# The second layer's output projection cut in eight weight units, the DeltaNet half of it placed inside the GLA norm chain

## The chip, the core and the metric

The kernel runs as one program on one core of a Trainium2 chip. The metric is the device time of one execution in us. The engines are PE (TensorE, matrix multiplication), DVE (VectorE), ACT (ScalarE), POOL (GpSimd) and SP (SyncE, which here only issues DMAs). Each runs its own instruction list in order and waits on semaphores for the others.

## The reference, cut to what matters

A decoder trunk of two layers runs once on 272 prompt tokens (16 meta tokens and 256) and on 8 sample groups of 4 tokens; the kernel puts them side by side as T = 304 columns. Layer 0 mixes with retention and mLSTM and has a gated feed-forward block. Layer 1 mixes with gated DeltaNet (heads "c") and GLA (heads "d"), projects both through one matrix `w_out1`, and ends with a mixture of experts, top 2 of 8:

```python
def _mixer_odd(x, state, segments, p):
    proj = x @ p['w_in1']
    qkv_c, z_c, b_c, a_c, q_d, k_d, v_d, r_d, lr_d = _split(proj, SPLITS1)
    ...
    o_c, s_gdn = _run_segments(_gdn_step, s_gdn, (qc, kc, vc, beta, g), segments)
    y_c = _merge(_head_norm(o_c, p['gdn_norm_g'], rms=True)) * jax.nn.silu(z_c.astype(f32))
    ...
    o_d, s_gla = _run_segments(_gla_step, s_gla, (qd, kd, vd, _heads(log_alpha, HD)), segments)
    y_d = _merge(_head_norm(o_d, p['gla_norm_g'])) * jax.nn.silu(r_d.astype(f32))
    y = jnp.concatenate([y_c, y_d], -1).astype(x.dtype) @ p['w_out1']

    # in _trunk, layer 1:
    x = _layer_norm(ALPHA * x + h, p['ln1_mix_g'], p['ln1_mix_b'])
    f = _moe(x, p['moe_w_router'], p['moe_b_router'], p['moe_w_gate'], p['moe_w_up'], p['moe_w_down'])
```

The final states of DeltaNet and GLA are outputs too, for the prompt and for every sample group.

## The kernel before

Activations are held as feature rows by token columns: 8 blocks of 128 features, 304 columns. Large products are done in a split form: ACT copies an operand to a "hi" part in a reduced type, DVE subtracts it from the raw one to give a "lo" part, and PE adds three matmuls (hi·hi, lo·hi, hi·lo; L612 to L614 in the helper `mm3`). So every weight tile passes SP (DMA), ACT (hi), DVE (lo) and PE in that order. The whole order of the program is written out by hand, engine by engine; nothing schedules it. Semaphores carry short names: `g_` is DeltaNet, `l_` GLA, `b_` the second output projection, `n1m_` the layer norm after it, `u_` a weight unit of the experts.

Layer 1 goes through these places. In the input projection PE takes 28 weight units of 24 matmuls (loop `unit1`), with the steps of DeltaNet's triangular solve between them. Then DeltaNet's outputs are formed (`g_o`) and evicted; `norm("g_", ...)` on DVE and ACT makes its 4 rows of `mix`, while PE makes four products for the new states, and DVE's `state_update` (one TENSOR_TENSOR L2025 and two L2027) adds each to the state. GLA follows: transposes of values (`l_vt`, copied to `vtl`) and keys (`l_kt`, to `ktl`), scores (`l_qk`), masked by DVE to `attl`, chunk products (L1163, L1166), from which DVE makes the running sums `sc` (L2481, L2483, signal `l_sc`), and four outputs (L1177 to L1182). They are evicted, and the GLA norm chain begins: head means on PE (L715), centring on DVE, squares on ACT, head variances on PE (L722), logarithm and exponential on ACT, gain on DVE, split to hi and lo. Between these PE does the four GLA state products (L1193), and DVE adds them (`l_update`, L2491 and L2493).

Only then comes the output projection: `w_out1` in two groups of 2 MB in `wring`, split into four `w_parts` of 2048 words each, 192 matmuls for 8 feature blocks with all 8 blocks of `mix` as input. `residual1` adds the old x (L2157), the layer norm sums on PE (L731), subtracts the mean (L2164), squares on ACT (L1470), sums again (L739), and the router starts (L1209). ACT copies the first two units, `for n in range(2): unit_hi(n)` (L1656), ahead of `layer_norm("n1m_", False)`.

The experts' weights are loaded by SP in units of 1.4 MB into five buffers. The first needs all earlier stores out of the way:

```python
            sp.wait_ge(*at("l_out", 1))
            sp.wait_ge(*at("st_all", 16 * 18))
```

The last of these 18 stores is that of the GLA states, which POOL issues (L1823) after `l_stu` 4, DVE's fourth `l_update`.

## Time and profile before

| what | value |
|---|---|
| time of the runs | 1535.31 us median of 3 (1535.15 to 1537.86) |
| profiled execution, its own time | 1540.06 us |
| its span in the trace | 1538.2 us |
| PE busy | 1418.4 us (92%) |
| DVE, ACT, POOL busy | 977.4, 744.9, 240.2 us |
| granted PE clock, mean | 0.924 of full speed |

A busy share is an average over stages with different limits; what a change in one stage is worth is read from the waits in that stage. "[1.67 <-ACT zT L1630]" at the end of a timeline row says that the engine was idle 1.67 us before it, and what it waited for. A PEclk of 1.00 is 2.4 GHz, 0.50 is 1.2 GHz.

### The profile page before, as it was taken

The numbers are of one execution on the slowest core, as the hardware profiler recorded it, in microseconds if no ns is written. First come the engines' busy times: TensorE is split into PE (matmuls) and PEld (weight loads), VectorE is DVE, ScalarE is ACT, GpSimd is POOL, SyncE is SP. The second block draws the span as 40 slices with busy tenths as digits, with TensorE's granted clock in tenths as the row PEclk, the third lists the DMA queues.
The fourth block names the chain that finished last, engine by engine and source line by source line (L and its number), as shares of the span: only waits on it lengthen the run. The fifth ranks groups of instructions, "written<-read, shape, count | busy, mean of one in ns | idle before, by whom it ended". The sixth has DMA issues, their size and how long they took to land.

```text
span 1538.2 us, 18458 instructions
## 1 busy us (share of the span) xinstructions
PE 1418.4 (92%) x7933; PEld 1237.4 (80%) x7933; DVE 977.4 (64%) x939; ACT 744.9 (48%) x622; POOL 240.2 (16%) x166
## 2 busy tenths in 40 slices
PE   7999999799999889998898766999999999999994
PEld 6898886799999678997686655887888888888882
DVE  4434465554553658743526556687988888788886
ACT  4434322432332566312303335566777778677771
POOL 0210302000000000001212040000000103356452
PEclk9999987899999989997657868999999999999998
DMA  7422624645424122202223437898999995400003
GB/s 256 144 95 83 231 96 140 201 129 177 147 83 144 46 83 83 87 29 56 68 76 103 176 133 282 309 382 334 377 396 377 387 375 213 160 28 14 15 14 98
DMA packets 80890, 254.81 MB, mean 166 GB/s; under 512 B 11568, under 2 KB 47700, under 8 KB 68008
## 3 DMA queue, kind: packets, MB, share of 16 engines
q1 hardware_dynamic: 66008, 224.53, 40.1%
q0 software_dynamic: 14800, 29.10, 6.2%
q8 instruction: 63, 1.03, 0.3%
q14 instruction: 19, 0.16, 0.0%
HBM read 306.09 MB, written 16.70 MB: 210 GB/s over the span
## 4 chain that ended last, share of the span: by engine, by line
PE 80%; DVE 7%; ACT 5%; DMA 5%; issue 2%; POOL 0%; POOLq 0%; SPq 0%; DVEq 0%; ACTq 0%
PE PS L612 11%; PE PS L614 10%; PE PS L613 10%; PE PS L1271 7%; PE PS L1273 7%; PE PS L1276 7%; DMA u_raw<-in_w_moe 4%; PE PS L592 3%; PE PS L1294 3%; PE PS L1295 3%; PE PS L1298 3%; PE PS L1008 2%; ACT u_hi L1656 1%; PE PS L677 1%; PE PS L1182 1%
## 5 line engine op out<-in xcount | busy, mean ns | idle before, releaser
L2508 DVE TENSOR_TENSOR u_lo<-u_raw,u_hi 128x2816 fp32r<-128x2816 f32 x144 | 441.9, 3089 | 110.1 <-ACT u_hi L1656 109.7
L1656 ACT ACTIVATE u_hi<-u_raw 128x2816 fp32r<-128x2816 f32 x144 | 367.7, 2561 | 183.4 <-DMA u_raw<-in_w_moe 114.4
L612 PE MATMUL PS<-x_in_hi,p_hi 128*128 128x304 f32 x480 | 158.1, 329 | 10.6 <-DVE x_in_lo L1898 10.5
L613 PE MATMUL PS<-x_in_lo,p_hi 128*128 128x304 f32 x480 | 148.1, 309 | 0.0
L614 PE MATMUL PS<-x_in_hi,p_lo 128*128 128x304 f32 x480 | 148.1, 309 | 0.0
L1271 PE MATMUL PS<-u_hi,xg_hi 128*128 128x512 f32 x576 | 142.6, 380 | 5.5 <-DVE xg_lo L2587 3.1
L1273 PE MATMUL PS<-u_hi,xg_lo 128*128 128x512 f32 x576 | 141.6, 378 | 0.0
L1276 PE MATMUL PS<-u_lo,xg_hi 128*128 128x512 f32 x576 | 140.2, 375 | 0.0
L612 PE MATMUL PS<-x_out_hi,w_parts 128*128 128x304 f32 x416 | 128.2, 308 | 9.4 <-DVE x_out_lo L1898 9.4
L614 PE MATMUL PS<-x_out_hi,w_parts 128*128 128x304 f32 x416 | 127.2, 306 | 0.0
L613 PE MATMUL PS<-x_out_lo,w_parts 128*128 128x304 f32 x416 | 126.7, 305 | 0.0
L1271 PEld LDWEIGHTS PS<-u_hi,xg_hi 128*128 128x128 f32 x576 | 103.4, 191 | 28.1 <-DVE xg_lo L2587 3.9
L1844 POOL DMA_INDIRECT u_raw<-in_w_moe,wpick x48 | 108.8, 2267 | 105.9 <-PE PS L1276 75.1
L1913 DVE TENSOR_TENSOR p_lo<-p_raw,p_hi 128x1024 fp32r<-128x1024 f32 x40 | 50.1, 1257 | 113.4 <-ACT p_hi L1358 113.4
L1273 PEld LDWEIGHTS PS<-u_hi,xg_lo 128*128 128x128 f32 x576 | 102.5, 190 | 21.6
L1276 PEld LDWEIGHTS PS<-u_lo,xg_hi 128*128 128x128 f32 x576 | 101.6, 188 | 21.1
L1294 PE MATMUL PS<-u_hi,ht_hi 128*128 128x512 f32 (+1 forms) x288 | 107.9, 378 | 1.2 <-issue 1.2
L612 PEld LDWEIGHTS PS<-x_in_hi,p_hi 128*128 128x128 f32 x480 | 94.1, 196 | 17.8 <-DVE x_in_lo L1898 10.5
L1295 PE MATMUL PS<-u_hi,ht_lo 128*128 128x512 f32 (+1 forms) x288 | 106.7, 374 | 0.0
L613 PEld LDWEIGHTS PS<-x_in_lo,p_hi 128*128 128x128 f32 x480 | 94.3, 196 | 0.4
L614 PEld LDWEIGHTS PS<-x_in_hi,p_lo 128*128 128x128 f32 x480 | 93.7, 195 | 0.0
L612 PEld LDWEIGHTS PS<-x_out_hi,w_parts 128*128 128x128 f32 x416 | 79.8, 192 | 11.5 <-issue 8.8
(545 smaller groups left out, 2501.6 us busy)
## 6 DMA issues: line engine op xcount, KB each, us to landing
u_raw<-in_w_moe SPq DMA_DIRECT2D x96, 1408.0 KB, 8.5
p_raw<-in_w_first SPq DMA_DIRECT2D x40, 512.0 KB, 3.5
p_raw<-in_w_second SPq DMA_DIRECT2D x28, 512.0 KB, 3.5
dring<-in_ffn_w_down SPq DMA_DIRECT2D x8, 1408.0 KB, 6.8
wring<-in_ffn_w_gate SPq DMA_DIRECT2D x9, 1024.0 KB, 5.6
wring<-in_ffn_w_up SPq DMA_DIRECT2D x9, 1024.0 KB, 8.1
wring<-in_w_out SPq DMA_DIRECT2D x2, 2048.0 KB, 7.7
o_rows<-zT POOLq DMA_DIRECT2D x6, 512.0 KB, 5.7
```

The costliest lines, as they stand in the source:

```text
L612: mm(out, w[0], x[0], start=start, stop=False)
L613: mm(out, w[0], x[1], start=False, stop=False)
L614: return mm(out, w[1], x[0], start=False, stop=stop)
L1271: mm(PSf[:, a:a + w], x_hi, w_hi[:, a:a + w], start=k == 0, stop=False)
L1273: mm(PSf[:, a:a + w], x_lo, w_hi[:, a:a + w], start=False, stop=False)
L1276: last = mm(PSf[:, a:a + w], x_hi, w_lo[:, a:a + w], start=False, stop=k == GUK - 1)
L1294: mm(o, h[0][:, j, :], w_hi[:, a:a + w], start=j == 0, stop=False)
L1295: mm(o, h[1][:, j, :], w_hi[:, a:a + w], start=False, stop=False)
L1656: A(uhi[n % HIS][:], uraw[n % RAW][:], COPY).then_inc(s("u_hi"), 1)
L1844: pool.indirect_dma_start(uraw[n % RAW][:], None, w_rows, bass.IndirectOffsetOnAxis(ap=wpick[:, o, u:u + 1], axis=0), bounds_check=NE * UP ...
L1913: TT(plo[n % PRAW][:], praw[n % PRAW][:], phi[n % PHI][:].bitcast(F32), SUB).then_inc(s("a_lo"), 1)
L2508: TT(ulo[n % RAW][:], uraw[n % RAW][:], uhi[n % HIS][:].bitcast(F32), SUB).then_inc(s("u_lo"), 1)
```

## The change

The second projection now goes in 8 units of 24 matmuls. The first four (n = 0 to 3) take blocks 0 to 3 of `mix` (DeltaNet), are placed by `first_half` between the PE steps of the GLA norm chain, and are added to x by DVE at once (`partial1`). The last four take blocks 4 to 7 (GLA) and stand where the projection stood. The units have their own raw buffers `oraw` (four in `arena`, four in `wring`), which is why GLA's `ktl`, `vtl` and `attl` leave `arena`. The 12 value transposes and their copies move from the DeltaNet states into the input projection (n = 25, 26). The key transposes and scores use other PSUM banks, and stand among the DeltaNet state products. DVE's wait for the store of the DeltaNet prompt state (`st_gp`) moves from the GLA masks to the residual. The four GLA outputs now wait for both halves of the running sums.

```diff
+        orw_at = [a_at + 1024 * r for r in range(4)] + [wring_at + 4096 + 1024 * r for r in range(4)]
+        ohi_at = [st_at + 6144, st_at + 7168, a_at + 4096]
+        oraw = [nc.alloc_sbuf_tensor_at(f"o_raw{n}", [128, KT, 128], F32, offset=SBUF0 + 4 * at_) for n, at_ in enumerate(orw_at)]
+        olo = [split(f"o_lo{n}", at_, [128, KT, 128]) for n, at_ in enumerate(orw_at)]
+        ohi = [split(f"o_hi{n}", at_, [128, KT, 128]) for n, at_ in enumerate(ohi_at)]
...
-        ktl = carve(arena, 6080, 768, 3, 256)
-        vtl = carve(arena, 6848, 1536, 3, 512)
-        attl = carve(arena, 8384, HT, 4, T)
+        ktl = carve(wring, 1216, 768, 3, 256)
+        vtl = carve(cst, N1 + 7, 1536, 3, 512)
+        attl = carve(wring, 1984, HT, 4, T)
...
-        GPAIRS = [(4, 7), (5, 7), (0, 1), (2, 3)]
+        GPAIRS = [(4, 7), (4, 7), (0, 1), (2, 3)]
...
-        LCHUNK = [(1, 2, 3), (4, 5, 6)]
-        LPAIRS = [(4, 5), (6, 7), (0, 1), (2, 3)]
-        LNB = {"n0m_": 2, "n0f_": 0, "n1m_": 4}
+        LCHUNK = [(2, 3, 4), (5, 0, 1)]
+        LQK = [5, 4, 0, 1]
+        OUTB = [6, 7, 0, 1, 2, 3, 4, 5]
+        LPAIRS = [(4, 5), (0, 1), (2, 3), (4, 5)]
+        LNB = {"n0m_": 2, "n0f_": 0, "n1m_": 6}
...
+            def out1(n):
+
+                if n % NHALF == 0:
+                    sp.wait_ge(*at(("g_o", "l_qk")[n // NHALF], 4))
+                if n >= NHALF:
+                    sp.wait_ge(*at("b_hi", n - NHALF + 1))
+                sp.dma_start(oraw[n][:], I["w_second"][NU1 + n]).then_inc(s(f"b_ld{n % NHALF}"), 16)
...
             for n in range(RAW):
-                if n == RAW - 1:
-                    sp.wait_ge(*at("b_lo", 4))
+                if n < NHALF:
+                    sp.wait_ge(*at("b_hi", NHALF + n + 1))
                 unit_load(n)
...
+            def out1(n, bank, free, between=None):
+
+                w, x = (ohi[n % 3], olo[n]), xsplit["out"]
+                pe.wait_ge(*at("b_lo", n + 1))
+                for j in range(2):
+                    d = 2 * (n % NHALF) + j
+                    pe.wait_ge(*free(d))
+                    for k in range(4):
+                        kx = k + (4 if n >= NHALF else 0)
+                        last = mm3(PS[:, bank(d), 0:T], [w[0][:, 4 * j + k, :], w[1][:, 4 * j + k, :]], [x[0][:, kx, :], x[1][:, kx, :]], k == 0, k == 3)
...
+                    last.then_inc(s("b_pe"), 1)
...
+                if n == 25:
+                    pe.wait_ge(*at("g_tok_d", 6))
+                    pe.wait_ge(*q_evicted(23))
+                    for i in range(2):
+                        tokens(4 + i, i, 20).then_inc(s("l_vt"), 1)
+                if n == 26:
+                    pe.wait_ge(*at("l_tok", 1))
+                    tokens(4, 2, 20).then_inc(s("l_vt"), 1)
             pe.wait_ge(*at("q_ev", len(REST)))
             pe.wait_ge(*at("sv_ev", len(ORDER)))
-            pe.wait_ge(*at("g_tok_d", 6))
+            pe.wait_ge(*at("l_tok", 3))
...
-            pe.wait_ge(*at("g_stu", 2))
-            for i, b in enumerate((4, 5, 7)):
-                tokens(b, i, 20).then_inc(s("l_vt"), 1)
-            pe.wait_ge(*at("g_stu", 4))
-            pe.wait_ge(*at("l_tok", 1))
-            pe.wait_ge(*at("l_dqk", 1))
-            for i, (a, n) in enumerate(TILES):
-                for p in range(2):
-                    last = tr(PS[0:n, 3 + i // 2, 256 * (i % 2) + 128 * p:256 * (i % 2) + 128 * p + 128], k2[:, p, a:a + n], 128)
-            last.then_inc(s("l_kt"), 1)
-            pe.wait_ge(*at("l_tok", 6))
...
+            def first_half(n):
+                out1(n, lambda d: 6 + d % 2, lambda d: at("b_ev", d - 1) if d >= 2 else at(*(("g_pst", 1), ("g_stu", 2))[d]))
+
            g_state(0)
+            head_vars("g_")
+            pe.wait_ge(*at("g_stu", 1))
+            g_state(1)
+            pe.wait_ge(*at("l_dqk", 1))
+            pe.wait_ge(*at("g_rstd", 1))
+            g_state(2)
+            for i, (a, n) in enumerate(TILES):
+                if i == 2:
+                    pe.wait_ge(*at("g_stu", 2))
+                for p in range(2):
+                    last = tr(PS[0:n, 5 - i // 2, 256 * (i % 2) + 128 * p:256 * (i % 2) + 128 * p + 128], k2[:, p, a:a + n], 128)
+            last.then_inc(s("l_kt"), 1)
+            g_state(3)
+            pe.wait_ge(*at("l_tok", 6))
+            l_scores(0)
+            l_scores(1)
+            pe.wait_ge(*at("g_stu", 3))
+            l_scores(2)
+            l_scores(3)
+            pe.wait_ge(*at("l_vb0", 1))
+            pe.wait_ge(*at("g_stu", 4))
+            pe.wait_ge(*at("l_att", 2))
+            l_chunks(0)
+            pe.wait_ge(*at("l_att", 4))
+            l_chunks(1)
+            pe.wait_ge(*at("ld_stG", 32))
+            pe.wait_ge(*at("l_sc", 2))
+            for h in range(H):
+                l_out(h)
+            head_means("l_")
+            pe.wait_ge(*at("xlo", 9))
+            first_half(0)
+            head_vars("l_")
+            first_half(1)
+            l_state(0)
+            first_half(2)
+            pe.wait_ge(*at("l_rstd", 1))
+            l_state(1)
+            first_half(3)
+            l_state(2)
+            pe.wait_ge(*at("l_stu", 1))
+            l_state(3)
+
+            OUTF = [at("b_ev", 7), at("b_ev", 8)] + [at("l_stu", 2)] * 2 + [at("l_stu", 3)] * 2 + [at("l_stu", 4)] * 2
             pe.wait_ge(*at("xlo", 10))
-            group(0, xsplit["out"], lambda t: [at("l_stu", 2)])
-            group(1, xsplit["out"], lambda t: [at("l_stu", 4)], between=mean_between("n1m_", 4 * GEND))
-            ln_sum("n1m_", [6, 7], "b_ev", 4 * GEND)
+            for n in range(NHALF, 2 * NHALF):
+                out1(n, lambda d: OUTB[d], lambda d: OUTF[d])
+                if n == 7:
+                    ln_sum("n1m_", range(4), "b_ev", 16)
+            ln_sum("n1m_", range(4, KT), "b_ev", 16)
...
+            def out1_hi(n):
+
+                act.wait_ge(*at(f"b_ld{n % NHALF}", 16 * (n // NHALF + 1)))
+                if n == 2:
+                    act.wait_ge(*at("g_state_pe", 4))
+                if n >= 3:
+                    act.wait_ge(*at("b_pe", 2 * (n - 2)))
+                A(ohi[n % 3][:], oraw[n][:], COPY).then_inc(s("b_hi"), 1)
...
+            def value_tokens(i):
+                n = TILES[i][1]
+                act.wait_ge(*at("l_vt", i + 1))
+                A(vtl[0:n, i, :], PS[0:n, 4 + i % 2, :], COPY).then_inc(s("l_tok"), 1)
...
+                if n == 26:
+                    act.wait_ge(*at("st_conv", 16))
+                    value_tokens(0)
+                    value_tokens(1)
+            value_tokens(2)
...
+            out1_hi(0)
...
-            for i, (a, n) in enumerate(TILES):
-                act.wait_ge(*at("l_vt", i + 1))
-                A(vtl[0:n, i, :], PS[0:n, (4, 5, 7)[i], :], COPY).then_inc(s("l_tok"), 1)
             act.wait_ge(*at("l_kt", 1))
             for i in range(3):
                 n = TILES[i][1]
-                A(ktl[0:n, i, :], PS[0:n, 3 + i // 2, 256 * (i % 2):256 * (i % 2) + 256], COPY).then_inc(s("l_tok"), 1)
+                A(ktl[0:n, i, :], PS[0:n, 5 - i // 2, 256 * (i % 2):256 * (i % 2) + 256], COPY).then_inc(s("l_tok"), 1)
+            out1_hi(1)
             x_hi("out", 0, mix, at("g_out", 1))
+            out1_hi(2)
             for h in range(H):
                 act.wait_ge(*at("l_o", h + 1))
                 A(zT[:, h, :], PS[:, h, 0:T], COPY).then_inc(s("l_oev"), 1)
-            norm("l_", lambda: proj_hi(0))
+            norm("l_", lambda: out1_hi(3))
+            out1_hi(4)
             x_hi("out", 1, mix, at("l_out", 1))
-            act.wait_ge(*at("l_state_pe", 4))
-            proj_hi(1)
-            proj_hi(2)
-            proj_hi(3)
+            for n in range(5, 2 * NHALF):
+                out1_hi(n)
...
+            def out1_lo(n):
+
+                dve.wait_ge(*at("b_hi", n + 1))
+                TT(olo[n][:], oraw[n][:], ohi[n % 3][:].bitcast(F32), SUB).then_inc(s("b_lo"), 1)
+
+            def partial1(d):
+                dve.wait_ge(*at("b_pe", d + 1))
+                STT(xT[:, d, :], xT[:, d, :], ALPHA, PS[:, 6 + d % 2, 0:T], MUL, ADD).then_inc(s("b_ev"), 1)
...
-                for u in range(4):
-                    if u < 2:
-                        proj_lo(2 + u)
-                    for k in (2 * u, 2 * u + 1):
-                        g = k // 4
-                        dve.wait_ge(*at("b_pe", 4 * g + k % 4 + 1))
-                        STT(zT[:, k, :], xT[:, k, :], ALPHA, PS[:, 4 * ((g + 1) % 2) + k % 4, 0:T], MUL, ADD).then_inc(s("b_ev"), 1)
+                for d in range(KT):
+                    dve.wait_ge(*at("b_pe", 9 + d))
+                    TT(zT[:, d, :], xT[:, d, :], PS[:, OUTB[d], 0:T], ADD).then_inc(s("b_ev"), 1)
...
-            norm("g_", 0, 12, "gdn", rms=True, prepare=lambda: g_update(0))
-            for h in range(1, H):
-                g_update(h)
+            norm("g_", 0, 12, "gdn", rms=True, prepare=lambda: (g_update(0), out1_lo(0)))
+            g_update(1)
+            x_lo("out", 0, mix, 9)
+            out1_lo(1)
+            g_update(2)
+            g_update(3)
...
-                if h == 0:
-                    dve.wait_ge(*at("st_gp", 16))
...
+            for h in range(H):
+                l_att(h)
+            out1_lo(2)
+            l_chunks(0)
+            l_chunks(1)
...
-            x_lo("out", 0, mix, 9)
-            norm("l_", 4, 24, "gla", prepare=lambda: (l_update(0), proj_lo(0)))
+            def before_rstd():
+                partial1(0)
+                partial1(1)
+                out1_lo(3)
+                partial1(2)
+                partial1(3)
+
+            norm("l_", 4, 24, "gla", prepare=before_rstd)
+            l_update(0)
+            x_lo("out", 1, mix, 10)
+            partial1(4)
+            partial1(5)
+            out1_lo(4)
             l_update(1)
-            x_lo("out", 1, mix, 10)
+            partial1(6)
+            partial1(7)
+            out1_lo(5)
             l_update(2)
             l_update(3)
-            proj_lo(1)
+            out1_lo(6)
+            out1_lo(7)
+            dve.wait_ge(*at("st_gp", 16))
```

On DVE, at the DeltaNet states: before, the second to fourth state update (L2025, L2027) stand one behind the other, and the prompt state (L2462) follows; the masks come after it. `stA` is the DeltaNet state, `vb`, `stu` and the like in brackets are the semaphores waited for.

```order
L2025 TENSOR_TENSOR stA<-stA,arena 128x8x128 [waits state_pe]
L2027 TENSOR_TENSOR stA<-stA,PS 128x4x128 [waits dve_chain]
L2027 TENSOR_TENSOR stA<-stA,PS 128x4x128
L2025 TENSOR_TENSOR stA<-stA,arena 128x8x128 [waits state_pe]
L2027 TENSOR_TENSOR stA<-stA,PS 128x4x128 [waits dve_chain]
L2027 TENSOR_TENSOR stA<-stA,PS 128x4x128
L2025 TENSOR_TENSOR stA<-stA,arena 128x8x128 [waits state_pe]
L2027 TENSOR_TENSOR stA<-stA,PS 128x4x128 [waits dve_chain]
L2027 TENSOR_TENSOR stA<-stA,PS 128x4x128
L2462 SCALAR_TENSOR_TENSOR arena<-arena,PS 128x128 x4
```

Now the split of `mix` (L1938) and of a weight unit of the projection (L1943) stand between the second update and the third:

```order
L2069 TENSOR_TENSOR stA<-stA,arena 128x8x128 [waits state_pe]
L2071 TENSOR_TENSOR stA<-stA,PS 128x4x128 [waits dve_chain]
L2071 TENSOR_TENSOR stA<-stA,PS 128x4x128
L1938 TENSOR_TENSOR x_out_lo<-mix,x_out_hi 128x1216 [waits xhi]
L1943 TENSOR_TENSOR o_lo_94<-o_raw_86,o_hi_102 128x1024 [waits hi]
L2069 TENSOR_TENSOR stA<-stA,arena 128x8x128 [waits state_pe]
L2071 TENSOR_TENSOR stA<-stA,PS 128x4x128 [waits dve_chain]
L2071 TENSOR_TENSOR stA<-stA,PS 128x4x128
L2069 TENSOR_TENSOR stA<-stA,arena 128x8x128 [waits state_pe]
L2071 TENSOR_TENSOR stA<-stA,PS 128x4x128 [waits dve_chain]
L2071 TENSOR_TENSOR stA<-stA,PS 128x4x128
L2505 SCALAR_TENSOR_TENSOR arena<-arena,PS 128x128 x4
```

The third and fourth update, the prompt state and the masks moved behind L1938, which waits for ACT (`xhi`).

On PE, in the same place: before, the last two DeltaNet state products (L1130, L1132) are followed by value transposes (`cc,proj`) and key transposes (`cc,wring`).

```order
L1130 MATMUL PS<-dring,arena 128x128 [waits vb,rstd]
L1132 MATMUL PS<-dring,arena 128x512 x2
L1130 MATMUL PS<-dring,arena 128x128 [waits vb]
L1132 MATMUL PS<-dring,arena 128x512 x2
L592 MATMUL PS<-cc,proj 128x128 [waits stu]
L592 MATMUL PS<-cc,proj 128x128 x7
L592 MATMUL PS<-cc,proj 48x128 x4
L592 MATMUL PS<-cc,wring 128x128 [waits l_dqk,tok_act,stu]
L592 MATMUL PS<-cc,wring 128x128 x3
L592 MATMUL PS<-cc,wring 48x128 x2
L1153 MATMUL PS<-wring 128x128 [waits tok_act]
```

Now the key transposes stand ahead of the fourth state product, and the last two wait for a state update (`stu`):

```order
L1132 MATMUL PS<-dring,arena 128x128 [waits vb,rstd,l_dqk]
L1134 MATMUL PS<-dring,arena 128x512 x2
L594 MATMUL PS<-cc,wring 128x128 x4
L594 MATMUL PS<-cc,wring 48x128 [waits stu]
L594 MATMUL PS<-cc,wring 48x128
L1132 MATMUL PS<-dring,arena 128x128 [waits vb]
L1134 MATMUL PS<-dring,arena 128x512 x2
L1141 MATMUL PS<-wring 128x128 [waits tok_act]
```

So ACT's key copies, which stand ahead of `xhi` on ACT, wait for the second state update.

On ACT, from the GLA norm to the layer norm: before, one copy of `mix` (L1343), three weight parts (L1351) and two expert units (`u_hi`, L1656) stand ahead of the layer norm's squares (L1470).

```order
L1456 ACTIVATE zT<-zT 128x1216 [waits act_chain]
L1343 ACTIVATE x_out_hi<-mix 128x1216 [waits out]
L1351 ACTIVATE w_parts<-wring 128x2048 [waits ring0,state_pe]
L1351 ACTIVATE w_parts<-wring 128x2048 [waits proj_pe,ring1] x2
L1656 ACTIVATE u_hi_98<-u_raw_88 128x2816 [waits fill0,proj_pe]
L1656 ACTIVATE u_hi_99<-u_raw_89 128x2816 [waits fill1]
L1470 ACTIVATE mix<-zT 128x608 [waits normcent] x4
```

Now it is five weight units (`o_hi`, L1382) and the same two expert units, ahead of the squares (L1501):

```order
L1487 ACTIVATE zT<-zT 128x1216 [waits act_chain]
L1382 ACTIVATE o_hi_102<-o_raw_89 128x1024 [waits proj_pe,fill0]
L1373 ACTIVATE x_out_hi<-mix 128x1216 [waits out]
L1382 ACTIVATE o_hi_103<-o_raw_90 128x1024 [waits proj_pe,fill1]
L1382 ACTIVATE o_hi_101<-o_raw_91 128x1024 [waits proj_pe,fill2]
L1382 ACTIVATE o_hi_102<-o_raw_92 128x1024 [waits proj_pe,fill3]
L1696 ACTIVATE u_hi_117<-u_raw_107 128x2816 [waits fill0,proj_pe]
L1696 ACTIVATE u_hi_118<-u_raw_108 128x2816 [waits fill1]
L1501 ACTIVATE mix<-zT 128x608 [waits normcent] x4
```

The two expert units still stand directly ahead of the squares; the copies before them became shorter and more.

## Rows read from the trace of the kernel before

**Rows 1.** Windows of all engines: stretch, length, busy (count) each, PEclk, DMA share, GB/s.
```profile
660.00:692.00 32.00, 31.61 (x253) 31.19 (x251) 13.55 (x19) 5.31 (x9) 0.09 (x1) 1.00 0.05 17
782.00:808.00 26.00, 25.84 (x119) 25.50 (x119) 4.78 (x11) 1.27 (x3) 0.00 (x0) 0.51 0.02 7
833.60:860.40 26.80, 26.80 (x187) 26.27 (x187) 11.01 (x12) 3.83 (x2) 3.66 (x5) 1.00 0.84 295
876.00:892.00 16.00, 16.00 (x84) 15.40 (x84) 6.71 (x28) 3.49 (x6) 0.00 (x0) 0.51 0.12 48
```

**Rows 2.** Timeline of PE, input projection: start us, us, engine, line, operation, tiles, [idle before].
```profile
649.60 1.31 PE L592 MATMUL PS<-cc,mix 128*128 128x128 f32 x12
...
692.12 1.28 PE L1079 MATMUL PS<-proj,arena 16*128 16x304 f32 x4 [0.51 <-ACT proj L1604]
```

**Rows 3.** Timeline of ACT, copies at the DeltaNet states.
```profile
765.63 0.59 ACT L1635 ACTIVATE arena<-PS 48x512 f32<-48x512 f32 x1 [0.24 <-PE PS L592]
768.60 0.91 ACT L1639 ACTIVATE arena<-PS 128x256 f32<-128x256 f32 x3 [2.38 <-PE PS L592]
769.41 1.21 ACT L1343 ACTIVATE x_out_hi<-mix 128x1216 fp32r<-128x1216 f32 x1
```

**Rows 4.** Timeline of DVE, from the second DeltaNet state update to the running sums.
```profile
761.44 1.28 DVE L2027 TENSOR_TENSOR stA<-stA,PS 128x512 f32<-128x512 f32 x2
...
767.55 1.11 DVE L2462 SCALAR_TENSOR_TENSOR arena<-arena,PS 128x128 f32<-128x128 f32 x4
773.24 0.42 DVE L2471 TENSOR_TENSOR arena<-PS,cst 128x256 f32<-128x256 f32 x1 [4.58 <-DMA out_prompt_gdn<-arena]
...
778.39 0.59 DVE L2481 COPY dring<-PS 64x128 f32<-64x128 f32 x2 [2.32 <-PE PS L1166]
...
785.81 1.43 DVE L1898 TENSOR_TENSOR x_out_lo<-mix,x_out_hi 128x1216 fp32r<-128x1216 f32 x1
```

**Rows 5.** Timeline of POOL, behind the DeltaNet prompt state.
```profile
769.96 1.05 POOL L1810 TENSOR_TENSOR dring<-arena,cst 48x512 f32<-48x512 f32 x1
```

**Rows 6.** Timeline of PE, from the GLA chunks to the head variances.
```profile
775.43 2.08 PE L1163 MATMUL PS<-arena 64*128 64x256 f32 x8
...
782.16 1.54 PE L1177 MATMUL PS<-arena 48*128 48x48 f32 x6 [2.06 <-DVEq L2485]
...
808.43 4.40 PE L715 MATMUL PS<-zT,cc 128*128 128x304 f32 x8
...
815.59 2.31 PE L722 MATMUL PS<-zT,cc 128*128 128x304 f32 x8 [0.63 <-ACT zT L1452]
817.83 1.98 PE L1193 MATMUL PS<-dring,arena 48*128 48x512 f32 x4
```

**Rows 7.** Timeline of DVE, the GLA gain, state updates three and four.
```profile
823.85 1.87 DVE L2014 SCALAR_TENSOR_TENSOR mix<-zT,vec,proj 128x304 f32<-128x304 f32 x4
...
829.68 1.21 DVE L2491 TENSOR_TENSOR stB<-stB,proj 64x1024 f32<-64x1024 f32 x1
...
833.49 1.30 DVE L2493 TENSOR_TENSOR stB<-stB,PS 64x512 f32<-64x512 f32 x2
```

**Rows 8.** SP's issue of the second expert unit.
```profile
843.63 0.81 SPq L568 DMA_DIRECT2D u_raw<-in_w_moe  x1
```

**Rows 9.** DMA issues by line at 843.6: queue, count, KB, median us to landing.
```profile
u_raw<-in_w_moe SPq DMA_DIRECT2D x1, 1408.0 KB, 9.3
```

**Rows 10.** Timeline of ACT, expert units behind the projection.
```profile
860.61 4.99 ACT L1656 ACTIVATE u_hi<-u_raw 128x2816 fp32r<-128x2816 f32 x2 [13.42 <-PE PS L614]
```

**Rows 11.** Timeline of PE, layer norm to the router.
```profile
860.41 2.21 PE L731 MATMUL PS<-zT,cc 128*128 128x304 f32 x8
866.25 4.36 PE L739 MATMUL PS<-mix,cc 128*128 128x304 f32 x16 [3.63 <-ACT mix L1470]
875.97 6.10 PE L1209 MATMUL PS<-proj,xT 128*128 128x8 f32 x32 [5.35 <-DVE xT L2176]
```

**Rows 12.** The page's DMA issues: tiles, queue, count, KB each, median us to landing.
```profile
p_raw<-in_w_second SPq DMA_DIRECT2D x28, 512.0 KB, 3.5
```

More of the change, by code:

```diff
@@ L556, in _ @@
                 unit1(n)
-            for g in range(GEND):
-                group(g)
+            for n in range(2 * NHALF):
+                out1(n)
             def unit_load(n):
@@ L667, in out_unit @@
                     last.then_inc(s("a_pe"), 1)
+                    if between is not None:
+                        between(4 * j + 3)
+            def out1(n, bank, free, between=None):
[7 more added lines that the diff above has]
+                        last = mm3(PS[:, bank(d), 0:T], [w[0][:, 4 * j + k, :], w[1][:, 4 * j + k, :]], [x[0][:, kx, :], x[1][:, kx, :]], k == 0, k == 3)
+                        if between is not None and k < 3:
+                            between(4 * j + k)
+                    last.then_inc(s("b_pe"), 1)
                     if between is not None:
```

93 lines of the change are left out of this document (22 added, 71 removed).

## The prediction

> **What bounds the kernel now.** I read the profile page first, then the chain that ended last, windows, and the timelines of each engine. All rows are from one execution of 1540.06 us; the runs have their median at 1535.31 us, 4.75 us less. Sums below are differences in that execution and are carried to the median unchanged.
>
> Up to 692 us PE is the bound of the input projection: 31.61 of 32 us busy at full clock [rows 1]. Anything put on PE there is paid in full, and its end hands over to ACT and back with 0.51 us idle [rows 2]. Then the chain goes through small steps in which PE, ACT and DVE wait for one another [rows 3 to 6]: the end of the DeltaNet states on DVE, a DMA wait of 4.58 us before the GLA masks, chunk products, running sums, and at 782.16 the four GLA outputs. These take until 808.43, 26.3 us on PE alone, at a clock of 0.51 [rows 1, 6]. From 808.43 the GLA norm chain alternates between engines, the states are updated [rows 7], and the projection keeps PE busy until 860.4 [rows 1]. Beside it SP loads the first expert units, the second at 843.63, landed after 9.3 us [rows 8, 9]; ACT copies two of them when the projection ends [rows 10], then squares for the layer norm, and PE sums [rows 11]. What comes later moves with that point.
>
> I follow one mark: the start of the layer norm's second sums on PE, 866.25 (L739). Write H for the start of the head means (L715): now 808.43, so the mark is at H + 57.8.
>
> **The change part by part.**
>
> *Transposes sooner.* 12 value transposes go into the input projection. 12 of the same form took 1.31 us there [rows 2]. ACT's copy of the third value tile, 0.59 us [rows 3], now stands between the last eviction and PE's L1079, which waits for it. Cost 1.9 us. Their old place was a gap of PE before the state updates ended, so taking them out of it gives nothing by itself.
>
> *DVE among the DeltaNet states.* The second update ends at 761.44 + 1.28 = 762.7 [rows 4]. Now PE waits for it with the last two key transposes (0.3 us, between 0.11 each at full clock [rows 2] and double), ACT copies the keys (0.91), one weight unit (1.0, from 1.21 us for 1216 columns to 1024) and `mix` (1.21) [rows 3], with handovers at 0.1: DVE is idle for 3.7 us. It then splits `mix` (1.43 us [rows 4]) and a unit (1.2, by 1024/1216). Together 6.3 us before the third update, which followed at once before. The prompt state ended at 767.55 + 1.11 = 768.66 and ends at 775.0.
>
> *Masks, chunks, sums.* The masks no longer wait for the DMA, 4.58 us [rows 4]; what is late next is POOL's value block, behind the issue of the prompt state's store. It ended at 769.96 + 1.05 = 771.0 [rows 5], 2.35 after the prompt state: now 777.35. DVE's masks and one unit (four pairs from 775.0 at about 0.5 each, and 1.2) end at 778.2, beside that. From the chunk products' start at 775.43 [rows 6] to the sums at 778.39 [rows 4] took 2.96 us: now 780.3. The outputs started after the first half of the sums; now they wait for both, which take until the 785.81 row [rows 4], 7.4 us: now 787.7 instead of 782.16 [rows 6], 5.5 late. With the 1.9 above, the outputs and H are 7.4 us late. The outputs themselves are unchanged.
>
> *Projection inside the norm chain.* A unit of 24 matmuls costs 3.3 us: 26.80 us held 187 instructions, 8 of them sums that took about 2.2 us (rows 11 show such a group), leaving 24.6 us for 179 [rows 1, 11]. Head means are 4.4, head variances 2.25, a GLA state product 2.0 [rows 6]. On PE: 4.4 + 3.3 + 2.25 + 3.3 + 2.0 + 3.3 + 2.0 = H + 20.6. The fourth unit then waits for DVE's `partial1`(4). The variances start at H + 7.7, and the gain's end came 10.1 after their start, 823.85 + 1.87 - 815.59 [rows 6, 7]: H + 17.8. Behind it DVE has a state update (1.21 + 1.30 = 2.5 [rows 7]), the split of `mix` (1.43) and the partial sum (0.5): H + 22.2. PE: that unit 3.3, two state products 4.0, H + 29.5, then four units, the last matmul at H + 42.7. Now it is at 860.4 = H + 52.0. Eight sums come after it, twice 2.21 [rows 11]: the mean is there at H + 47.1.
>
> *What decides: the fourth GLA update.* From H + 22.2 DVE does another partial sum, a unit, an update, two partial sums, a unit, then updates three and four: 0.5 + 1.2 + 2.5 + 1.0 + 1.2 + 5.0 = H + 33.6. Before, it ended at 833.49 + 1.30 = 834.8 = H + 26.4 [rows 7]. Behind it are queued POOL's store of the GLA states, SP's wait for all stores, and the expert loads. The second unit landed at 843.63 + 9.3 = 852.9, 18.1 after the update [rows 8, 9]; now H + 51.7. ACT copies it, half of 4.99 [rows 10], until H + 54.2; the squares stand behind that. Before, the copies ended at 865.6 = H + 57.2, and PE followed 0.65 later [rows 10, 11]. So the mark comes 3.0 earlier after H, not the 9 that the projection frees. Net 7.4 - 3.0 = 4.4 us later.
>
> *The clock at the mark.* PE is then idle from H + 47.1 to H + 54.8, 7.7 us; now it is 3.63 us, and the 16 sums ran at full clock in 4.36 [rows 11]. After an idle time of 5.35 the next stretch ran at 0.51 [rows 1, 11]. By the first row the sums cost nothing more; all at half clock they would cost 4.4 more, since 8 took 4.40 at the head means [rows 6]. I take 2.2: the first 8 at half clock, the rest full, as the head means and what followed them did. The Trainium skill ("TensorE: Matmul & The Clock Gate", section "What's actually happening") says that the default state is throttled and that activity releases the throttle. By that rule the sums start at half clock; the row of 5.35 agrees, the row of 3.63 does not show it.
>
> Edits at nothing: the four early weight loads (the same form lands after 3.5 us [rows 12]; as late as 9.3, as an expert unit [rows 9], they would delay DeltaNet's norm by up to 5.8; nothing else is queued there, and before 745 nothing waits for them, so no gain: I take 0); DVE's `st_gp` wait at the residual (the store is long done); banks and places in memory. The copies of units five to eight lie beside PE's units.
>
> Sum: 1.9 + 5.5 - 3.0 + 2.2 = +6.6 us: 1546.7 in the profiled execution, 1541.9 by the median.
>
> **The rivals.**
>
> 1. *Expert units are not in the way* (not slower). If the second unit lands 11.8 us after the fourth update instead of 18.1, the squares follow the mean at once: 47.1 + 0.7 for the subtraction + 0.7 for a square = H + 48.5 instead of 57.8. Then 7.4 - 9.3 = -1.9, 1533.4 us. For it speaks that the DMA queues are nearly idle in that stretch; against it that the store, its wait and the 9.3 us are all measured. It decides below a landing of about 14 us.
> 2. *The GLA outputs run at full clock* (faster): half of 26.3 us, 13.1, would go: 1528.8. Dense matmuls come before and after; but the outputs followed dense work before as well and stayed at 0.51 [rows 1].
> 3. *No loss of clock* at the mark: +4.4, 1539.7.
> 4. *More at half clock*: the first unit behind the head means (3.3 more) and all 16 sums (2.2 more): +12.1, 1547.4.
> 5. *The half is not hidden*: PE does not fit it between the chain's steps, since the chain waits for PE more than PE for it. That is in my sum for H + 22.2; if DVE were never late there, updates would end 1.6 sooner, 1540.3.
>
> **How the numbers follow.** Forecast with its own spread (rival 5 within it) 0.47; rival 3 0.18; rival 4 0.12; rival 1 0.16; rival 2 0.07. Below 0.2%, 3.1 us, a measurement of this kernel can't be told from no change. Slower by more: the forecast, rival 4 and most of rival 3, 0.75. Faster by more: rival 2 and a part of rival 1, 0.11. Within: 0.14. The range 1533.0 to 1546.5 takes in rival 1 and most of rival 4; the slower cases alone give 1538.5 to 1546.5.
>
> **What would show it.** Right: DVE idle about 3.7 us before the split of `mix` among the DeltaNet states; the outputs 7 us later; the last projection matmul about 43 us after H; ACT waiting for an expert unit's DMA before its squares, PE idle over 6 us there and then at half clock. Wrong: outputs less than 5 us late; squares that follow the mean at once; a clock over 0.6 in the outputs.

## The result, and the profile after

The changed kernel takes 1548.61 us, median of 15 runs (1540.4 to 1556.25); the kernel before, run beside it, 1535.45 us, median of 15 (1529.9 to 1542.26). The ratio is 1.0079, 95% interval 1.0061 to 1.0096, which is 9.4 to 14.7 us more. The forecast was +6.6 us: the sign was right, the size about half, and the time lies above the range.

The profiled execution of the changed kernel took 1556.25 us, its span is 1554.4 us. It is not read against the span before as it stands: executions of one kernel differ by several us ahead of 650 us, in stages that the change leaves alone (the 12 transposes that start the table stand at 649.60 and 644.87 us in two executions of the kernel before). The stretches below are differences within each execution. The column "before" has two executions of that kernel, the one shown above and the run `b0_before_again`.

| stretch, from and to | before | after | difference | forecast |
|---|---|---|---|---|
| 12 DeltaNet transposes in the projection [rows 2] to L1079 (after: L1085) | 42.52, 42.52 | 44.29 | +1.8 | +1.9 |
| DVE's first operation on that result to ACT's copy of the DeltaNet outputs | 51.68, 51.69 | 52.95 | +1.3 | 0 |
| to the end of the second DeltaNet update | 17.60, 17.60 | 17.92 | +0.3 | 0 |
| to the start of the GLA outputs | 19.43, 19.43 | 27.11 | +7.7 | +5.5 |
| to H, the head means | 26.27, 26.27 | 26.51 | +0.2 | 0 |
| H to DVE's scaling behind the layer norm's second sums | 64.45, 64.49 | 66.99 | +2.5 | -0.8 |
| to the first expert matmul | 37.69, 37.58 | 37.68 | 0 | 0 |
| to the end | 627.64, 621.85 | 622.44 | 0 | 0 |

The sum is 13.8 us, inside the interval of the runs. It counts the last stretch as unchanged. The two executions of before differ by 5.8 us there (in the longer one ACT waits 3.9 us more for the experts' loads), and in the eleven traces of the changed kernel and of the variants below the stretch takes 621.0 to 625.5 us, so 627.64 is the odd one.

DVE between the second update and the running sums, in the changed kernel (start us, us, engine, line, operation, tiles, [idle before <- what ended it]):

```profile
777.41 1.43 DVE L1938 TENSOR_TENSOR x_out_lo<-mix,x_out_hi 128x1216 fp32r<-128x1216 f32 x1 [3.71 <-ACT x_out_hi L1373]
778.75 1.22 DVE L1943 TENSOR_TENSOR o_lo<-o_raw,o_hi 128x1024 fp32r<-128x1024 f32 x1
...
784.80 1.12 DVE L2505 SCALAR_TENSOR_TENSOR arena<-arena,PS 128x128 f32<-128x128 f32 x4
...
787.62 5.86 DVE L1943 TENSOR_TENSOR o_lo<-o_raw,o_hi 128x1024 fp32r<-128x1024 f32 x1
793.40 0.58 DVE L2522 COPY dring<-PS 64x128 f32<-64x128 f32 x2
```

The first two rows are the wait and the splits as forecast, against [rows 4], where the third update followed at once. The fourth row was not: a split of 1.22 us takes 5.86 us. POOL in the same place, and the chunk products on PE:

```profile
787.21 1.05 POOL L1850 TENSOR_TENSOR dring<-cst 48x512 f32<-48x512 f32 x1
788.20 4.18 POOL L1856 TENSOR_TENSOR dring<-cst 48x1152 f32<-48x1152 f32 x2
```

```profile
788.31 2.08 PE L1147 MATMUL PS<-cst,wring 64*128 64x256 f32 x8 [2.83 <-POOL dring L1850]
...
790.82 0.42 PE L1150 MATMUL PS<-dring,wring 48*128 48x128 f32 x1
```

The split ends at 793.48, which is 1.1 us after POOL's blocks end at 792.38: it looks as if it stood still until POOL was through, which the third experiment tests. The first half of the chunk products ends on PE at 791.24 (790.82 + 0.42), and the sums that read it start at 793.40, so the split delays them by some 2 us. The GLA outputs then follow (compare [rows 6]):

```profile
800.81 1.78 PE L1160 MATMUL PS<-wring,cst 48*128 48x48 f32 x6 [7.01 <-DVEq L2526]
```

The same happens twice in the norm chain. DVE, then POOL, behind H, which is 827.32 here:

```profile
842.61 3.60 DVE L2058 SCALAR_TENSOR_TENSOR mix<-zT,vec,proj 128x304 f32<-128x304 f32 x4
...
848.59 1.41 DVE L1938 TENSOR_TENSOR x_out_lo<-mix,x_out_hi 128x1216 fp32r<-128x1216 f32 x1
...
850.68 1.21 DVE L1943 TENSOR_TENSOR o_lo<-o_raw,o_hi 128x1024 fp32r<-128x1024 f32 x1
851.92 3.03 DVE L2538 TENSOR_TENSOR stB<-stB,proj 64x1024 f32<-64x1024 f32 x1
...
862.02 1.30 DVE L2540 TENSOR_TENSOR stB<-stB,PS 64x512 f32<-64x512 f32 x2
```

```profile
842.31 2.23 POOL L1856 TENSOR_TENSOR dring<-cst 48x1152 f32<-48x1152 f32 x1 [49.93 <-PE PS L1172]
847.76 6.10 POOL L1856 TENSOR_TENSOR dring<-cst 48x1152 f32<-48x1152 f32 x1 [3.22 <-PE PS L1172]
```

The gain takes 3.60 us where [rows 7] have 1.87, an update's product 3.03 where they have 1.21; POOL's own block, 2.23 us in the first row, takes 6.10 in a stretch in which DVE runs two splits of 1.41 and 1.21 us in their usual time. So of such a pair either side can be the one that is held up. The fourth update ends at H + 36.0.

The end of the stretch: SP's expert loads, ACT's copies of them ahead of the squares, and PE's mean and second sums.

```profile
871.69 2.60 SPq L570 DMA_DIRECT2D u_raw<-in_w_moe  x5
```

```profile
879.54 2.55 ACT L1696 ACTIVATE u_hi<-u_raw 128x2816 fp32r<-128x2816 f32 x1 [14.98 <-DMA u_raw<-in_w_moe]
882.87 2.55 ACT L1696 ACTIVATE u_hi<-u_raw 128x2816 fp32r<-128x2816 f32 x1 [0.78 <-DMA u_raw<-in_w_moe]
885.32 2.50 ACT L1501 ACTIVATE mix<-zT 128x608 f32<-128x608 f32 x4
```

```profile
873.24 4.25 PE L733 MATMUL PS<-zT,cc 128*128 128x304 f32 x16
886.07 5.98 PE L741 MATMUL PS<-mix,cc 128*128 128x304 f32 x16 [8.57 <-ACT mix L1501]
```

The mean is there at H + 50.2, 4 us sooner than before, but ACT waits for two loads, and the squares start at H + 58.0, 0.9 later than before. [Rows 10, 11] showed 4.99 us of copies without a wait between, 3.63 us of idle PE and 4.36 us of sums.

Granted clock, over the 13 us behind the input projection and over the second sums (stretch, length, busy and count of PE, of PE's weight loads, of DVE, ACT and POOL, then PEclk, DMA share, GB/s). Before:

```profile
693.45:706.45 13.00, 9.01 (x59) 8.32 (x60) 5.91 (x10) 2.72 (x5) 0.17 (x1) 0.87 0.59 162
866.20:870.70 4.50, 4.36 (x16) 2.96 (x16) 4.50 (x2) 3.13 (x6) 0.00 (x0) 1.00 0.00 0
```

After, with the outputs and the first and the fourth projection unit behind H between them:

```profile
702.83:715.83 13.00, 9.88 (x56) 8.95 (x56) 5.22 (x9) 2.72 (x5) 0.00 (x0) 0.74 0.58 162
800.81:827.32 26.51, 26.51 (x120) 26.09 (x121) 0.00 (x0) 1.27 (x3) 0.00 (x0) 0.50 0.00 1
831.08:834.94 3.86, 3.86 (x27) 3.77 (x26) 1.89 (x2) 1.22 (x1) 0.00 (x0) 0.97 0.00 0
850.52:856.16 5.64, 5.64 (x24) 5.47 (x24) 5.57 (x5) 0.00 (x0) 4.57 (x3) 0.58 0.12 26
886.00:892.10 6.10, 5.98 (x16) 3.95 (x16) 2.54 (x1) 3.12 (x6) 0.00 (x0) 0.72 0.70 299
```

The outputs stay at half clock, as in [rows 1]. New is the lower clock right behind the input projection, 0.74 instead of 0.87; the +1.3 us of the table lies there. New is also the fourth unit: PE has to wait for DVE ahead of it, and then it takes 5.64 us where the first one took 3.86:

```profile
850.52 0.59 PE L614 MATMUL PS<-x_out_hi,o_hi 128*128 128x304 f32 x1 [2.84 <-DVE xT L1947]
```

### The profile page after: what moved, and what is told of

Same layout as the page of the kernel before. It is cut to its first block, busy times and chain, and to the rows that moved or that the text cites. A ratio compares the mean times of both kernels' runs of the same rounds, so it can differ in the third digit from the quotient of the medians.

```text
span 1554.4 us, 18491 instructions
## 1 busy us (share of the span) xinstructions
PE 1427.6 (92%) x7933; PEld 1244.0 (80%) x7933; DVE 989.7 (64%) x951; ACT 746.2 (48%) x626; POOL 253.5 (16%) x166
## 4 chain that ended last, share of the span: by engine, by line
PE 78%; DVE 9%; DMA 6%; ACT 5%; issue 2%; POOL 0%; POOLq 0%; SPq 0%; DVEq 0%; ACTq 0%
PE PS L614 10%; PE PS L616 9%; PE PS L615 9%; PE PS L1301 7%; PE PS L1303 7%; PE PS L1306 7%; DMA u_raw<-in_w_moe 4%; PE PS L594 3%; PE PS L1325 3%; PE PS L1328 3%; PE PS L1324 3%; PE PS L1006 2%; PE PS L679 1%; ACT u_hi L1696 1%; PE PS L741 1%
## 5 line engine op out<-in xcount | busy, mean ns | idle before, releaser
L1884 POOL DMA_INDIRECT u_raw<-in_w_moe,wpick x48 | 122.8, 2558 | 92.0 <-PE PS L1306 65.0
L1957 DVE TENSOR_TENSOR p_lo<-p_raw,p_hi 128x1024 fp32r<-128x1024 f32 x40 | 50.1, 1256 | 119.5 <-ACT p_hi L1389 119.5
L614 PE MATMUL PS<-x_out_hi,w_parts 128*128 128x304 f32 x352 | 107.5, 305 | 8.3 <-DVE x_out_lo L1938 8.3
L616 PE MATMUL PS<-x_out_hi,w_parts 128*128 128x304 f32 x352 | 107.1, 304 | 0.0
L615 PE MATMUL PS<-x_out_lo,w_parts 128*128 128x304 f32 x352 | 106.5, 303 | 0.0
L2224 DVE TENSOR_TENSOR w_parts<-wring,w_parts 128x2048 fp32r<-128x2048 f32 x20 | 45.8, 2292 | 67.5 <-ACT w_parts L1521 67.5
```

The source lines that it names most:

```text
L614: mm(out, w[0], x[0], start=start, stop=False)
L615: mm(out, w[0], x[1], start=False, stop=False)
L616: return mm(out, w[1], x[0], start=False, stop=stop)
L1884: pool.indirect_dma_start(uraw[n % RAW][:], None, w_rows, bass.IndirectOffsetOnAxis(ap=wpick[:, o, u:u + 1], axis=0), bounds_check=NE * UP ...
L1957: TT(plo[n % PRAW][:], praw[n % PRAW][:], phi[n % PHI][:].bitcast(F32), SUB).then_inc(s("a_lo"), 1)
```

## Experiments

The theories: A, the waits named in the prediction (DVE among the DeltaNet states, the sums, the expert units ahead of the squares); D, DVE and POOL in each other's way; K, clock lost elsewhere because the projection ends later. Ratios are to the kernel before, run beside them, whose median was 1535.1 to 1536.5 us in these runs; they are given with their 95% interval and are not the quotients of the two medians. Runs of one kernel lie up to 17 us apart, so what an edit did is read from the stretches inside a trace, and the time says whether it arrives.

**Splits behind the sums.** DVE's `x_lo` and two units go to where DVE is idle during the outputs.

```
             g_update(1)
-            x_lo("out", 0, mix, 9)
-            out1_lo(1)
             g_update(2)
...
-            out1_lo(2)
             l_chunks(0)
             l_chunks(1)
+            x_lo("out", 0, mix, 9)
+            out1_lo(1)
+            out1_lo(2)
```

> The changed kernel, with DVE's split of mix and its units two and three (L1938, L1943 x2) moved behind the running sums, where DVE is idle for 31 us. Theory A (DVE's wait of 3.7 us and these splits set the start of the GLA outputs): the third update follows the second one as soon as PE has the state products, the prompt state ends 3.9 us sooner (PE's product of head three, not DVE, is then late), the unit no longer stands between masks and sums for 5.86 us, the outputs start about 6 us sooner after the second update, and the time is 1548.6 - 6 = 1542.6 us. Rival B (POOL's value block or a load of the GLA states is late next): the outputs stay within 2 us of where they are, 1547 us or more.

1541.91 us, ratio 1.0032 (1.0013 to 1.0050). From the second update to the outputs it took 21.2 us instead of 27.1, 5.9 less where theory A said about 6; rival B falls. PE's wait ahead of the outputs fell from 7.01 us, and the rest of the gain lies before it:

```profile
781.42 1.78 PE L1160 MATMUL PS<-wring,cst 48*128 48x48 f32 x6 [4.90 <-DVEq L2524]
```

**Expert units behind the layer norm.** ACT's and DVE's splits of the first two expert units swap places with the norm.

```
             act.wait_ge(*at("b_pe", 16))
-            for n in range(2):
-                unit_hi(n)
             layer_norm("n1m_", False)
+            for n in range(2):
+                unit_hi(n)
...
-            layer_norm("n1m_", "mix1", lambda: [unit_lo(n) for n in range(2)])
+            layer_norm("n1m_", "mix1")
+            for n in range(2):
+                unit_lo(n)
```

> The changed kernel, with the two expert units split behind the layer norm on ACT and DVE instead of ahead of ACT's squares. Theory A (the load of the expert units behind the fourth GLA update holds the squares up by 7 us, and the idle time costs PE's clock at the mark): squares follow the mean within 1.5 us, the second sums take 4.4 instead of 6 us, the time is 8.6 us less, 1540.0 us. Rival C (the time is not lost there: the units' splits have to be paid later, beside the router, or the mixture waits for its weights all the same): 1545 us or more.

1541.4 us, ratio 1.0029 (1.0008 to 1.0050). From H to the scaling it took 58.42 us instead of 66.99: 8.57 less, and the first expert matmul came no later after it (36.9 us). PE's second sums:

```profile
868.41 4.36 PE L741 MATMUL PS<-mix,cc 128*128 128x304 f32 x16 [1.68 <-ACT mix L1501]
```

Of the 8.57, 7.0 are the wait and 1.6 the clock (the sums took 4.36 instead of 5.98). Rival C falls.

**POOL's blocks behind the sums.** Four buffers instead of two, all filled while DVE is idle.

```
-        lb = [carve(dring, 1280, 1152, SEGS, 128), carve(dring, 2432, 1152, SEGS, 128)]
+        lb = [carve(dring, 1280, 1152, SEGS, 128), carve(dring, 2432, 1152, SEGS, 128),
+              carve(dring, 4096, 1152, SEGS, 128), carve(arena, 6400, 1152, SEGS, 128)]
...
+            pool.wait_ge(*at("l_sc", 2))
             for h in range(H):
-                if h >= 2:
-                    pool.wait_ge(*at("l_state_pe", h - 1))
-                G.tensor_tensor(lb[h % 2][0:R2], ...
+                G.tensor_tensor(lb[h][0:R2], ...
```

> The changed kernel, with POOL's four wide value blocks (L1856) in four buffers and all made behind the running sums, while DVE is idle, instead of beside DVE's masks, gain and updates. Theory D (DVE's operations on SBUF alone stretch beside POOL's blocks: unit three 5.86 instead of 1.2 us, the gain 3.60 instead of 1.87, the second update's product 3.03 instead of 1.21): these take their short times, the sums start 2.1 us sooner, the fourth update comes 3.5 us sooner after the head means, the time is 5.6 us less, 1543.0 us. Rival E (they are long for another reason, such as where their data lies): their times stay, and so does the total, 1548.6 us within 1.5.

1544.58 us, ratio 1.0047 (1.0027 to 1.0067). DVE's three operations, the code and its place unchanged:

```profile
779.54 1.73 DVE L1942 TENSOR_TENSOR o_lo<-o_raw,o_hi 128x1024 fp32r<-128x1024 f32 x1
...
833.40 1.88 DVE L2057 SCALAR_TENSOR_TENSOR mix<-zT,vec,proj 128x304 f32<-128x304 f32 x4
...
840.98 1.22 DVE L2537 TENSOR_TENSOR stB<-stB,proj 64x1024 f32<-64x1024 f32 x1
```

5.86, 3.60 and 3.03 became 1.73, 1.88 and 1.22 (the first still stands beside POOL's L1850, 1.05 us). The outputs came 2.1 sooner, as expected. The fourth update came only 1.4 sooner after H, not 3.5: the projection's first unit behind the head means took 4.83 us instead of 3.86, at a granted clock of 0.76 instead of 0.97, and that ate 1.0; a partial sum on DVE then waited for PE's units, and with it the updates behind it, 1.2.

```profile
820.90:825.73 4.83, 4.83 (x27) 4.66 (x26) 1.89 (x2) 1.22 (x1) 0.00 (x0) 0.76 0.00 0
```

Theory D holds, its second size was too big, and the time fell by 4.0 us of the 5.6 expected. (The interval of this ratio still overlaps that of the changed kernel; the rows decide.) In the Trainium skill, "SBUF — State Buffer", section "SBUF: two separate sides", such a pair is foreseen: a DVE operation with two SBUF inputs and a GpSimd operation that reads SBUF exclude each other for a whole instruction. The rows agree: the three DVE operations that stretched have both inputs in SBUF, and took their short times with POOL's blocks gone. In the first experiment the copy that starts the running sums, which reads PSUM, ran wholly beside POOL's blocks (770.93 to 775.11 us) and took its usual time, as the blocks did:

```profile
774.00 0.59 DVE L2520 COPY dring<-PS 64x128 f32<-64x128 f32 x2 [2.83 <-PE PS L1150]
```

```profile
770.93 4.18 POOL L1856 TENSOR_TENSOR dring<-cst 48x1152 f32<-48x1152 f32 x2
```

**All three.**

> The changed kernel with the three edits of the runs beside it. If the three costs add (theories A and D): 6.0 less before the outputs, 3.5 less in the norm chain, 8.6 less at the mark, 1548.6 - 18.1 = 1530.5 us, under the kernel before. If the expert units or the mixture's weights are late again (rival C), 1537 us or more.

1530.79 us, ratio 0.9958 (0.9939 to 0.9976): the costs add (the three single edits took 6.7, 7.2 and 4.0 us off 1548.61, together 17.9; all three took 17.8), and the change with them removed is faster than the kernel before.

```profile
850.17 4.26 PE L733 MATMUL PS<-zT,cc 128*128 128x304 f32 x16
856.11 4.36 PE L741 MATMUL PS<-mix,cc 128*128 128x304 f32 x16 [1.68 <-ACT mix L1501]
```

H is 808.69 in this trace, so the mean is at H + 45.7, 8.5 sooner than before. That is what the projection inside the norm chain gives here once these costs are out of its way.

**The first half of the sums is enough.** On top of these, other banks for the second chunk products, so that the outputs need not wait for the second half.

```
-        LCHUNK = [(2, 3, 4), (5, 0, 1)]
+        LCHUNK = [(2, 3, 4), (5, 6, 7)]
...
             pe.wait_ge(*at("ld_stG", 32))
-            pe.wait_ge(*at("l_sc", 2))
```

> The version with the three edits (splits of mix and units behind the running sums, POOL's blocks behind them, expert units behind the layer norm), and with the second half of the chunk products in banks 5 to 7, so that the first two GLA outputs wait for the first half of the sums alone, as before the change. Theory A (the outputs wait for the second half of the sums, 3.7 us): 1530.8 - 3.7 = 1527.1 us. Rival B (another wait, for a load or for PE itself, is right behind): 1530 us or more.

1526.86 us, ratio 0.9946 (0.9927 to 0.9964), the lowest median of all. The stretch from the second update to the outputs fell from 21.2 to 17.6 us, by the 3.65 us of half the sums; the intervals of the two ratios overlap.

**The kernel before again, and with its expert units later.** The second has the same edit as the second experiment, on the kernel before.

> The kernel before, unchanged, for a second profile of it. In its first one the mixture of experts, from its first expert matmul to the end, took 627.6 us, in the changed kernel and its variants 621.8 to 622.8. Theory N (chance: two expert units landed late, and one clock stretch): about 622.5 us here too, so that nothing is given back after the layer norm. Rival G (the change gives some 5 us back there, by loads that start at another point): 626 us or more. The granted half clock after the input projection lasts 3.4 us here if its longer stretch in the variants comes from the change.

One run, 1529.44 us. The last stretch took 621.85 us: theory N. Its second sums took 4.36 us after 3.63 us of idle time, as in [rows 11].

> The kernel before, with the two expert units split behind the layer norm on ACT and DVE, as was done with the changed kernel. Theory A (there the loads hold the squares up by 7 us, here only ACT's copies do, by 2.1 us, and PE keeps its clock): squares follow the mean within 1 us, 1535.1 - 2.1 = 1533.0 us. Rival C (the edit gains the same 7 us in both kernels, so it says nothing on the change): 1528 us.

1534.32 us, ratio 0.9981 (0.9964 to 0.9998). H to the scaling fell by 1.9 us, from 64.5 to 62.6, against 8.57 in the changed kernel. So nearly all of the wait for the loads is a cost of the change.

**The transposes alone.** The kernel before with units 25 and 26, their copies and the buffer as changed, the rest as before; and once more with the transposes at both places.

```
+                if n == 25:
+                    pe.wait_ge(*at("g_tok_d", 6))
+                    pe.wait_ge(*q_evicted(23))
+                    for i in range(2):
+                        tokens(4 + i, i, 20).then_inc(s("l_vt"), 1)
+                if n == 26:
+                    pe.wait_ge(*at("l_tok", 1))
+                    tokens(4, 2, 20).then_inc(s("l_vt"), 1)
...
-            for i, b in enumerate((4, 5, 7)):
-                tokens(b, i, 20).then_inc(s("l_vt"), 1)
```

> The kernel before with one part of the change alone: the value transposes in units 25 and 26 of the input projection, their copies behind the evictions there, and the value tokens' buffer outside the arena. Theory A: the input projection ends 1.9 us later, a half clock stretch behind it is 3.4 us longer (1.3 us), and nothing is won later: 1535.1 + 1.9 to 3.2, 1537.0 to 1538.3 us. Rival F (the old place was on the path too): the keys' products come sooner, 1535 us or less.

1545.24 us, ratio 1.0068 (1.0043 to 1.0092): 8.8 us more by the medians, where I expected 1.9 to 3.2. The projection ends 1.8 us later and the stretch behind it takes 52.95 instead of 51.7, as expected. But the way from H to the scaling takes 69.24 us instead of 64.5, with nothing moved there. The head variances and the second sums in that run, and the clock behind the projection, at the variances and at the sums:

```profile
821.71 3.99 PE L722 MATMUL PS<-zT,cc 128*128 128x304 f32 x8 [0.85 <-ACT zT L1456]
...
874.30 7.27 PE L739 MATMUL PS<-mix,cc 128*128 128x304 f32 x16 [3.63 <-ACT mix L1474]
```

```profile
697.16:710.16 13.00, 9.88 (x56) 8.95 (x56) 5.22 (x9) 2.72 (x5) 0.00 (x0) 0.74 0.57 162
821.71:825.70 3.99, 3.99 (x9) 2.25 (x9) 3.89 (x4) 3.03 (x2) 2.38 (x1) 0.57 0.01 3
874.30:881.60 7.30, 7.27 (x16) 4.72 (x16) 5.29 (x2) 3.03 (x4) 0.00 (x0) 0.60 0.00 0
```

The idle time ahead of the sums is 3.63 us as in [rows 11]; there they took 4.36 us, here 7.27. The variances took 2.31 us in [rows 6], here 3.99.

> The kernel before with the value transposes and ACT's copies made twice, in units 25 and 26 of the input projection as in the change, and again at their old place (the same values over the same). It tells what in the run with the transposes alone moved the clock. Theory K1 (the later end of the input projection puts the half clock stretches elsewhere): as that run, some 9 us over before, 1545 us, with half clock for 6.8 us behind the projection. Rival K2 (their absence at the old place thins out PE's work there, and that lowers the clock later): only the 1.9 to 3.2 us of the projection's end, 1538 to 1540 us.

1540.15 us, ratio 1.0038 (1.0016 to 1.0061). The time is close to what rival K2 said (1538 to 1540), not to K1's 1545. The trace says otherwise: both costs are back, 52.95 us behind the projection and 69.08 from H to the scaling, with PE's old work in its place, so its absence there is not what lowers the clock in these two stretches. What makes the time lower is the way from the second update to H, 3.2 us shorter than with the transposes moved. Why it is shorter stays open, and with intervals that overlap the time doesn't decide between K1 and K2.

**The transposes back, in the changed kernel and in the best version.**

> The changed kernel with its value transposes taken out of the input projection again and put where the kernel before had them in spirit, among the DeltaNet state products (tiles through banks 5, 5 and 7), everything else as changed. Theory K (the transposes in the input projection cost 1.9 us themselves and some 7 us more by stretches of half clock that then fall on other work, as in the run with the transposes alone): 1548.6 - 9 + 1, since ACT's third copy stands ahead of the keys, 1540.6 us; half clock behind the input projection for 3.4 us again, not 6.8. Rival A (only the 1.9 us and the 1.3 us right behind the projection are the transposes', the rest of the loss is in the other parts): 1548.6 - 3.2 + 1, 1546.4 us.

1549.4 us, ratio 1.0083 (1.0053 to 1.0113): nothing is won. The clock behind the projection is as before, and so is the stretch there (51.82 us):

```profile
696.71:709.71 13.00, 9.01 (x58) 8.32 (x59) 5.91 (x10) 2.72 (x5) 0.17 (x1) 0.87 0.58 162
```

But the way from the second update to the outputs is 0.9 longer (28.02 us), with ACT's copy now ahead of the keys, and the gain ends at H + 19.8 instead of 18.9. Theory K as I put it, with some 7 us to win back, falls for the changed kernel. Rival A, 1546.4 us, is 3.0 under the median of these six runs and inside their interval.

> The version with all four edits (first half of the sums enough, splits and POOL's blocks behind the sums, expert units behind the layer norm) with the value transposes back among the state products. Theory K: its squares and sums already run at full clock, so fewer stretches are left to win; 1526.9 - 1.9 - 1.3 - 0.5 + 1 = 1524.2 us. Rival (they cost as much here as alone, 9 us): 1518.9 us. Rival (what they cost among the states, where ACT's copies stand ahead of the keys, is as much as in the projection): 1526.9 us.

1528.61 us, ratio 0.9945 (0.9924 to 0.9966), not to be told from the best version: the last rival, by which the transposes cost as much at either place.

## Why the prediction was wrong

The direction held, and so did four parts of the mechanism: DVE idle for 3.71 us and the splits at 1.43 and 1.22, the outputs at half clock, the expert units ahead of the squares, PE idle 8.57 us and then slow. The sum was 7 us short, in these steps:

- **"DVE's masks and one unit (four pairs ... and 1.2) end at 778.2, beside that"** is the step that failed first. I laid the unit beside POOL's value block and let it cost nothing, with a duration from rows in which POOL was idle. It took 5.86 us and held up the sums: +2.1, taken away by the third experiment. The trace of the kernel before had the sign of it: one and the same DVE operation, L2008, takes 1.82 us where it starts 0.54 us ahead of the end of a POOL block, and 1.42 where no POOL block runs (rows below). The first half of that path, the 6.3 us of DVE's wait and splits, is right.
- **"1.0 + 1.2 + 5.0 = H + 33.6"**, the fourth GLA update that decides, used durations without POOL again, for the gain and the second update: +1.7 and +1.8, less 1.1 that I had too much. Measured H + 36.0, +2.4.
- **"The second unit landed ... 18.1 after the update"** carried a landing of 9.3 us [rows 9] to the new place. ACT could start its copy only 19.6 us after it (882.87 - 863.32), +1.5: the unit was issued as long after the update as before, but landed 10.8 us after its issue. With both, +3.9, the largest error in the sum: the 3.0 us that this term gave back became a loss, from H the squares come 0.9 later than before. Rival 1, that they would not wait, was the wrong side of the same question; the second experiment prices the wait at 7.0 us.
- **The clock at the mark**, 2.2 in the sum, measured 1.6 (5.98 against 4.36). The size was near, the reason was not: the run with the transposes alone has the same 3.63 us of idle time as before and loses 2.9 us, so the idle time ahead alone doesn't tell the clock.
- **"Cost 1.9 us"** for the transposes was right as PE's and ACT's own time (+1.8). Missing was any term for the clock behind it: +1.3 in every kernel that has them there, and, without the rest of the change, 4.8 us more between H and the scaling. I bounded the clock only at the mark and at the first unit, so the range was too narrow.
- **"the last matmul at H + 42.7"** and the mean at H + 47.1 came 3.1 later, at H + 45.9 and H + 50.2. 1.0 of it is a longer wait for DVE's partial sum ahead of the fourth unit (H + 23.2 instead of 22.2), 2.3 the unit itself, which took 5.64 us at a granted clock of 0.58 instead of 3.3. In the changed kernel this is hidden behind the wait for the loads; with the expert units moved it is not (the mean is at H + 50.1 there), and with all three edits, where the fourth unit runs at full clock, it is gone.

DVE's L2008 in the trace of before, at both places, and the POOL block beside the first:

```profile
756.54 1.82 DVE L2008 TENSOR_TENSOR zT<-zT 128x1216 f32<-128x1216 f32 x1 [4.73 <-ACT zT L1630]
...
822.39 1.42 DVE L2008 TENSOR_TENSOR zT<-zT 128x1216 f32<-128x1216 f32 x1 [2.06 <-ACT zT L1456]
```

```profile
754.98 2.10 POOL L1797 TENSOR_TENSOR dring<-dring,cst 48x1152 f32<-48x1152 f32 x1 [2.52 <-PE PS L1132]
```

Rival 4, more at half clock, had nearly the time that came (1547.4) by the wrong way: the first unit behind the head means ran at full clock (3.86 us for 24 matmuls, 0.97), the fourth did not but was hidden, and not all 16 sums ran at half.

What stays open: which part of the loss by clock belongs to which edit. Each kernel has its own pattern; the transposes alone lose some 6 us by it (1.3 behind the projection, 4.8 behind H, of which 2.9 are in the second sums and 1.7 in the head variances), and taking them out of the changed kernel wins nothing. What in an edit moves the clock no run shows.
